# A two-layer recurrent and attention backbone: separate banks for the last gates, and output projections that open with the rounded parts of two row tiles

## The reference, cut to what matters

```python
# layer 0
z = h @ w_in                                   # (T, 1024) @ (1024, 2048)
g_ = gelu(z[..., :D]);  xc = conv4(z[..., D:])
for d in (0, 1):                               # forward, backward
    g = einsum('btnk,gnkj->gbtnj', xc_blocks, gate_w[d]) + gate_b[d]
    r, ig = sigmoid(g[0]), sigmoid(g[1])
    log_a = -8 * r * softplus(-lam[d])
    h_t = exp(log_a) * h_t-1 + sqrt(-expm1(2 * log_a)) * (ig * xc)
o = (sum_over_d(h) * g_) @ w_out
# layer 1
o = attention_heads(512 x 1024) @ w_o
# both
x = x + gate1 * o
hn = modulate(rmsnorm(x), shift, scale)
aff = softmax(hn @ router);  gate, idx = top_k(aff.T, cap)     # per expert
x = x + gate2 * scatter(gate * swiglu(hn[idx], w_up[e], w_down[e]))
```

## Time and profile before

| | before |
|---|---|
| median of 3 runs | 1846.26 us (1844.49 to 1847.72) |
| the profiled execution | 1847.21 us |
| its span in the profile | 1845.5 us |
| mean granted TensorE clock | 0.972 of 2.4 GHz |
| TensorE matmul busy | 1687.3 us (91%) |
| VectorE busy | 710.8 us (39%) |
| ScalarE busy | 528.3 us (29%) |
| loads and stores | 520.56 MB, mean 282 GB/s |
| last recurrent unit, first projection and choice of rows | 239 to 383 us of the span |
| experts of layer 0 | from 383 us |
| last attention values, second projection and choice | 1282 to 1377 us |
| experts of layer 1 | from 1377 us |

### The profile page before, as it was taken

One profiled execution on the slowest core, in us unless ns is written; L12 is line 12 of the kernel. 1 busy time (PEld: TensorE's weight loads), 2 busy tenths in 40 slices (PEclk: granted clock), 3 DMA queues, 4 the chain that ended last, 5 costly groups with the idle time before them and its releaser, 6 DMA issues. The chain is left out here.

```text
span 1845.5 us, 23947 instructions
## 1 busy us (share of the span) xinstructions
PE 1687.3 (91%) x9811; PEld 882.4 (48%) x9811; DVE 710.8 (39%) x1431; ACT 528.3 (29%) x885; POOL 181.1 (10%) x198
## 2 busy tenths in 40 slices
PE   4999989879999999999988999999959998888887
PEld 2667768533333333333358778777833332222222
DVE  4667765611221221221145655665451221122123
ACT  4677783300110110110144445446210000000002
POOL 1000010100001000010011225324000000000001
PEclk8999999979999999999999999999979999999999
DMA  9554351699999999999881000000579999999996
GB/s 360 190 206 163 140 220 64 263 386 407 397 404 391 399 403 385 403 404 385 342 300 50 22 1 0 0 0 34 210 308 421 421 420 422 421 421 421 421 422 258
DMA packets 89577, 520.56 MB, mean 282 GB/s; under 512 B 11347, under 2 KB 19648, under 8 KB 33936
## 3 DMA queue, kind: packets, MB, share of 16 engines
q1 hardware_dynamic: 80128, 487.74, 65.6%
q0 software_dynamic: 9360, 31.54, 5.5%
HBM read 502.37 MB, written 16.88 MB: 281 GB/s over the span
## 5 line engine op out<-in xcount | busy, mean ns | idle before, releaser
L847 PE MATMUL wide<-sb_ring_x,sb_xT 128*64 128x512 f32 x1160 | 266.6, 601 | 19.8 <-DMA sb_ring_x<-moe_w_up 18.7
L847 PE MATMUL wide<-sb_ring,sb_xT 128*64 128x512 f32 x888 | 204.5, 603 | 14.4 <-DMA sb_ring<-moe_w_up 12.2
L847 PEld LDWEIGHTS wide<-sb_ring_x,sb_xT 128*64 128x64 f32 x1160 | 78.0, 137 | 190.1 <-issue 136.9
L847 PEld LDWEIGHTS wide<-sb_ring,sb_xT 128*64 128x64 f32 x888 | 60.9, 138 | 146.3 <-issue 108.8
L902 PE MATMUL duo<-sb_ring_x,sb_hidT 128*64 128x512 f32 x536 | 124.3, 599 | 4.4 <-DMA sb_ring_x<-moe_w_down 4.4
L1832 DVE TENSOR_TENSOR sb_hid<-wide,sb_sg 128x512 f32<-128x512 f32 x16 | 11.1, 692 | 304.3 <-ACT sb_sg_c L1365 304.3
L2281 POOL TENSOR_TENSOR sb_prob<-sb_prob,sb_asum 128x768 f32<-128x768 f32 x64 | 93.9, 1468 | 186.4 <-DVE sb_asum L2105 186.4
L902 PE MATMUL duo<-sb_ring,sb_hidT 128*64 128x512 f32 x424 | 99.9, 601 | 7.2 <-DMA sb_ring<-moe_w_down 7.1
L1363 ACT ACTIVATE sb_sg<-wide 128x512 f32<-128x512 f32 x16 | 9.6, 597 | 335.7 <-PE wide L858 335.7
L1832 DVE TENSOR_TENSOR sb_hid<-wide,sb_hid 128x512 f32<-128x512 f32 x16 | 11.1, 691 | 227.1 <-ACT sb_hid L1363 227.1
L1363 ACT ACTIVATE sb_hid<-wide 128x512 f32<-128x512 f32 x16 | 9.6, 598 | 278.5 <-PE wide L847 278.5
(11 more groups left out here) (389 smaller groups left out, 2866.4 us busy)
## 6 DMA issues: line engine op xcount, KB each, us to landing
sb_ring_x<-moe_w_up SPq DMA_DIRECT2D x145, 1024.0 KB, 25.0
sb_ring<-moe_w_up SPq DMA_DIRECT2D x111, 1024.0 KB, 24.4
sb_ring_x<-moe_w_down SPq DMA_DIRECT2D x69, 1024.0 KB, 23.0
sb_ring<-moe_w_down SPq DMA_DIRECT2D x59, 1024.0 KB, 23.9
sb_ring<-ada_w SPq DMA_DIRECT2D x40, 1024.0 KB, 7.0
sb_ring<-lru_w_in SPq DMA_DIRECT2D x8, 1024.0 KB, 8.2
sb_ring_x<-ada_w SPq DMA_DIRECT2D x8, 1024.0 KB, 7.5
sb_ring<-lru_w_out SPq DMA_DIRECT2D x4, 1024.0 KB, 4.9
```

Source lines behind the costliest of these rows:

```text
L847: ins = mm(wide[n * CAPL:(n + 1) * CAPL, s, :], mine[:, k, :], w[:, at:at + BANK], start=k == 0, stop=k == KD - 1)
```

## The change

The last block's plan puts both gates ahead of its ada chunks. Unit 15's gates go to `wide` banks 2, 3 and 0, without waiting for unit 14's sigmoids (the last product waits for gelu 6, which reads bank 0), and the last input projection goes to the two banks of `turned`, after unit 14's sigmoids. The warming products are 20, not 46.

Both output projections begin with `first_two`: rounded by rounded products of tiles 0 and 1, block by block as rounded weights come; then the products of the row tiles' rests, tile 0 and tile 1; then those of the weights' rests, tile 0 and tile 1. The last block (two blocks in layer 1) of the rounded tiles is made apart, so that the others need not wait for the last Y (or heads). Product 2 is now cut in two, with tile 0's turning between; from product 3 on the order is as it was. The slots of the up projections are given back by turnings into `turned`, without the wait for the heads.

```diff
@@ plan @@
-        plan += [("gate", n, 0)] + beside[0:3] + [("gate", n, 1)] + beside[3:]
+        if n < KD - 1:
+            plan += [("gate", n, 0)] + beside[0:3] + [("gate", n, 1)] + beside[3:]
+        else:
+            plan += [("gate", n, 0), ("gate", n, 1)] + beside
@@
+        EARLY_K = [KD - 1, KD - 2]
+        def in_banks(p):
+            if p == 2 * KD - 1:
+                return turned[:, 0, :], turned[:, 1, 0:TC]
+            return wide[:, 2 * (p % 2), :], wide[:, 2 * (p % 2) + 1, 0:TC]
+
+        def gate_banks(u):
+            if u == 2 * KD - 1:
+                return wide[:, 2, :], wide[:, 3, :], wide[:, 0, :]
+            return turned[:, 0, :], turned[:, 1, :], duo[:, 0, :]
@@ in_project @@
-                if p >= 2:
+                if p == 2 * KD - 1:
+                    pe.wait_ge(s_sig, p)
+                elif p >= 2:
@@ gates @@
-                if u >= 1:
+                if 1 <= u < 2 * KD - 1:
                     pe.wait_ge(s_sig, u)
...
+                if u == 2 * KD - 1:
+                    pe.wait_ge(s_gelu, KD - 1)
+                mm(i_lat, w[:, KD + n, :], seg(xc, 0), start=True, stop=True).then_inc(s_gmm, 1)
@@ out_project @@
+                def first_two():
+                    lhs, w = [out_lhs(lay, t) for t in range(2)], [out_w(lay, k) for k in range(KD)]
+                    for k in range(KD):
+                        pe.wait_ge(s_whi, W0[lay] + k + 1)
+                        if k == EARLY_K[lay]:
+                            pe.wait_ge(s_hhi, L0[lay] + 2)
+                        for t in range(2):
+                            for n in range(2):
+                                mm(wide[:, 2 * t + n, :], lhs[t][1][:, k, :], w[k][1][:, n * BANK:(n + 1) * BANK], start=k == 0, stop=False)
+                    for t in range(2):
+                        pe.wait_ge(s_hlo, L0[lay] + t + 1)
+                        for k in range(KD):
+                            for n in range(2):
+                                mm(wide[:, 2 * t + n, :], lhs[t][2][:, k, :], w[k][1][:, n * BANK:(n + 1) * BANK], start=False, stop=False)
+                    for t in range(2):
+                        for k in range(KD):
+                            if t == 0:
+                                pe.wait_ge(s_wlo, W0[lay] + k + 1)
+                            for n in range(2):
+                                ins = mm(wide[:, 2 * t + n, :], lhs[t][1][:, k, :], w[k][2][:, n * BANK:(n + 1) * BANK],
+                                         start=False, stop=k == KD - 1)
+                        ins.then_inc(s_o[lay], 1)
...
+                first_two()
+                product(2, 0, 4)
+                turn_tile(s, 0)
+                product(2, 4, KD)
+                turn_tile(s, 1)
...
+                logit_products(0)
+                product(3, 0, KD)
+                turn_tile(s, 2)
+                logit_products(1)
+                turn_logits(0)
@@ after the plan @@
-            idle_products(duo[:, 0, :], 46)
+            idle_products(duo[:, 0, :], 20)
@@ after the attention loop @@
-            pe.wait_ge(s_OT, 2 * NG + 2)
...
-                turn(duo[0:32, 1, 32 * n:32 * n + 32], ident[0:32, 0:32]).then_inc(used[place[name][0]], 1)
+                turn(turned[0:32, 0, 32 * n:32 * n + 32], ident[0:32, 0:32]).then_inc(used[place[name][0]], 1)
@@ norm_and_logits, ScalarE @@
-                out_weights_hi(lay, 0, 1)
-                if lay == 0:
-                    act.wait_ge(s_yg, KD)
-                else:
-                    act.wait_ge(s_OT, 2 * NG + 2)
-                out_lhs_hi(lay, 0)
-                out_weights_hi(lay, *range(2, KD))
-                out_lhs_hi(lay, 1)
+                ready, last, early_w = ((s_yg, KD - 1), (s_yg, KD), 5) if lay == 0 else ((s_OT, 2 * NG), (s_OT, 2 * NG + 2), 3)
+                act.wait_ge(*ready)
+                for t in range(2):
+                    x_, hi, _ = out_lhs(lay, t)
+                    fn(hi[:, 0:EARLY_K[lay], :], x_[:, 0:EARLY_K[lay], :], ACT.Copy)
+                out_weights_hi(lay, *range(early_w))
+                act.wait_ge(*last)
+                for t in range(2):
+                    x_, hi, _ = out_lhs(lay, t)
+                    fn(hi[:, EARLY_K[lay]:KD, :], x_[:, EARLY_K[lay]:KD, :], ACT.Copy).then_inc(s_hhi, 1)
+                out_weights_hi(lay, *range(early_w, KD))
@@ residual_norm, VectorE @@
-                out_weights_lo(lay, 0)
+                out_weights_lo(lay, 0, 1)
                 out_lhs_lo(lay, 0)
-                out_weights_lo(lay, *range(1, KD))
                 out_lhs_lo(lay, 1)
+                out_weights_lo(lay, *range(2, KD))
```

More of the change, by code:

```diff
@@ L571, in idle_products, with ada_chunk @@
                     mm(bank[:, 0:P], ident[:], ident[:], start=True, stop=True)
-            def ada_chunk(i, k, owed=None):
+            def ada_chunk(i, k, *owed):
+                owed = [d for d in owed if d is not None]
                 if i >= 1 and k == 0:
@@ L583, in ada_chunk @@
                              start=k == 0, stop=k == KD - 1)
-                    if owed and n == 0:
-                        ins.then_inc(owed, 1)
+                    if n < len(owed):
+                        ins.then_inc(owed[n], 1)
                 ins.then_inc(used[place[("ada", i, k)][0]], 1)
@@ L638, in in_project @@
                 pe.wait_ge(s_wlo, p + 1)
-                b = 2 * (p % 2)
+                banks = in_banks(p)
                 for k in range(KD):
@@ L644, in in_project @@
                         for i in range(2):
-                            ins = mm(wide[:, b, :] if i == 0 else wide[:, b + 1, 0:TC], w[:, p % 2, k, :], seg(h[:, k, :], i),
+                            ins = mm(banks[i], w[:, p % 2, k, :], seg(h[:, k, :], i),
                                      start=k == 0 and n == 0, stop=k == KD - 1 and n == 2)
@@ L672, in _ @@
                 if what == "in":
-                    in_project(*at, last, owed)
-                    owed = None
+                    in_project(*at, last, *owed)
+                    owed = []
                 elif what == "gate":
                     gates(*at)
-                    owed = last
+                    if last is not None:
+                        owed.append(last)
                 elif what == "ada":
-                    ada_chunk(*at, owed)
-                    owed = None
+                    ada_chunk(*at, *owed)
+                    owed = []
                 else:
@@ L732, in turn_logits @@
                     turn(duo[:, 1, 0:P], logit_parts[:]).then_inc(s_logt, 1)
-                if lay == 0:
-                    for t in range(4):
-                        product(t, 0, KD)
-                        if t >= 1:
-                            turn_tile(s, t - 1)
-                        if t == 2:
-                            pe.wait_ge(s_modcol, 4)
-                        if t >= 2:
-                            logit_products(t - 2)
-                        if t == 3:
-                            turn_logits(0)
+                first_two()
[3 more added lines that the diff above has]
+                turn_tile(s, 1)
+                if lay == 0:
+                    pe.wait_ge(s_modcol, 4)
+                else:
+                    pe.wait_ge(s_OT, 2 * NG + 2)
+                logit_products(0)
[3 more added lines that the diff above has]
+                turn_logits(0)
+                if lay == 0:
                     product(4, 0, 4)
@@ L777, in out_project @@
                     return
-                for step in range(n_t + 3):
-                    if step < n_t:
-                        product(step, 0, KD)
-                    if 1 <= step <= n_t:
-                        turn_tile(s, step - 1, *(() if step < n_t else [used[place[names[3]][0]]] + [used[j] for j in WO_SLOTS]))
-                    if 2 <= step <= n_t + 1:
-                        logit_products(step - 2)
-                    if step >= 3:
-                        turn_logits(step - 3)
+                turn_tile(s, 3, *([used[place[names[3]][0]]] + [used[j] for j in WO_SLOTS]))
+                logit_products(2)
+                turn_logits(1)
+                logit_products(3)
+                turn_logits(2)
+                turn_logits(3)
             def turn_choice(lay):
@@ L1249, in _ @@
                         act.wait_ge(s_yg, (u - 3) // 2 + 1)
-                    for g, lat, dst in ((1, duo[:, 0, :], IT), (0, turned[:, 0, :], RT)):
+                    r_lat, ctx_, i_lat = gate_banks(u)
+                    for g, lat, dst in ((1, i_lat, IT), (0, r_lat, RT)):
                         bias = pB[:, B_GB + (2 * d + g) * KD + n:B_GB + (2 * d + g) * KD + n + 1]
                         fn(seg(dst[:, u % 3, :], 0), lat, ACT.Sigmoid, bias=bias)
-                        ins = fn(seg(dst[:, u % 3, :], 1), turned[:, 1, g * TC:(g + 1) * TC], ACT.Sigmoid, bias=bias)
+                        ins = fn(seg(dst[:, u % 3, :], 1), ctx_[:, g * TC:(g + 1) * TC], ACT.Sigmoid, bias=bias)
```

(6 more changed lines are left out.)

15 lines of the change are left out of this document (6 added, 9 removed).

## The result

The changed kernel takes **1834.91 us** (median of 4 runs, 1834.40 to 1835.16), beside it the kernel before took 1846.87 us; the ratio is 0.9937, interval 0.992 to 0.9954. Forecast were 1836.1 us and a range of 1833.5 to 1840.0. The profiled execution took 1835.05 us for a span of 1833.3.

The account below looks back on a forecast made before the run. No one engine bounds the kernel; expert stages start when the projections before them end, where engines wait in turn. 6.7 us (first layer) plus 3.5 (second) gives 10.2, so 1846.26 - 10.2 = 1836.1 us; range 1833.5 to 1840.0.

Parts of the forecast that it names:

- The bound: Both expert stages: neither is shortened, but each starts as much earlier as the output projection and choice of rows end.
- Nothing passes: Rival, both layers: the choices of rows wait for something other than the projection; time stays at 1846; chance 0.05.
- the second start being worth nothing: Rival, second layer's projection: none of its 3.5 us passes, gain 6.7 us, time 1839.6; chance 0.12.
- The last unit: Last recurrent unit: unit 15's sigmoids, waiting for Y of block 6, start at 249.87 not 252.59; 2.7 us, not 4.7.
- The first projection, its start: First layer's output projection: TensorE begins at 266.15, after the first rounded weight at 266.1, and follows ScalarE's pace.
- The wait before product 2: First layer's output projection: product 2 waits 0.2 us for tile 0's residual and tile 2's rest.
- The first projection, its clock: First projection: cutting warming products from 46 to 20 leaves a 2.6 us gap; clock loss taken as 0.
- the rival: Clock falls at the first projection, costing 1.1 us: gain 9.1 us, time 1837.2; chance 0.18.
- The second projection: Second layer's output projection: starts at 1285.6 not 1288.57, tile 1 turned 3.5 us earlier, 1.5 of it from the clock.
- The load of weight 6: Second projection: load of weights 6 and 7, issued 0.9 earlier and asked for at 1290.8, may cost some tenths.
- Slower: Rival, first projection: first pair runs at 1.2 GHz throughout, 12 us slower, 1858; chance 0.02.

Follow-up runs that it names:

- second projection alone: Kernel before with the new order only in the second layer's output projection, its five dummy turnings placed earlier, 46 warming products kept: 1841.64 us, ratio 0.9978.
- the gates alone: Kernel before with only the last unit's gate banks and order new, old projections and 46 warming products: 1841.51 us, ratio 0.9982.
- early sigmoids: Changed kernel, unit 15's sigmoids waiting for block 6's scan, not its Y; 20 warming products: 1831.05 us, ratio 0.9924; once more 1834.04 us, 0.993.
- the changed kernel's third: Changed kernel measured a third time, no edit: 1834.90 us, ratio 0.9942 to the kernel before.
- early sigmoids with 26: Changed kernel, unit 15's sigmoids waiting for block 6's scan instead of its Y, 26 warming products in place of 20: 1831.35 us, ratio 0.991.

## Why the prediction was right, and where not

**The bound.** Right: the gain passes through both expert stages. From the first up product of layer two to the end it is 468.1 before and 467.8 changed, 467.6 to 468.0 in all but two of the other profiles (469.3 and 469.4 in those). In the first layer the first up product came at 376.22 for 383.35, 7.1 earlier, of which 2.46 are the start. "Nothing passes" falls, and so does the second start being worth nothing, with 3.4 to 3.6 in it in each of the nine profiles of the new order without a late load.

**The last unit.** Right to some hundredths: 2.70 for 2.72 forecast, the sigmoids behind Y of block 6, and not the 4.7 that the gates alone would give. The run without this wait shows the other 2.1. The slow gate products that the prediction read in the earlier trace rows come with a fall of the clock: in all three profiles with the old gates it fell during TensorE's wait of 4.3 us there or just after it; with the new gates, whose last product waits 0.88 to 1.04, in none of ten.

**The first projection, its start.** Forecast were 16.28 us from the sigmoids to the first product, measured 16.33. The wait before product 2: 0.2 forecast, 0.18 measured. Without a fall of the clock the pair and product 2 take 34.95 (32 warming products) where 35.25 were forecast.

**The first projection, its clock.** This step failed, inside a forecast that came out right. I took 0 for the cut of the warming products, with the argument that the gap is a single one behind dense products, as that of 1.8 us is. The clock fell in all four profiles with a gap of 2.70 or 2.71, and the gap of 1.8 was no safe model either: with the second projection alone it fell behind that one too. It cost 1.1 us against 32 products, the number kept as the price of the rival (1.1). That rival had a chance of 0.18 and is what happened; its loss was made up by terms set a little too low (0.3 in the products, 0.1 in the second layer) and by scatter. The local parts alone would have given 1846.26 - 9.6 = 1836.7; that the median came out 1.2 below the forecast, and not 0.6 above it, is luck. The local parts give 9.6, the rival said 9.1, the forecast 10.2; the three measurements of the changed kernel gave 12.0, 9.1 and 10.9.
Counted over all profiles at this place, the clock was low at the first products once in one behind a gap of 7.17, four times in four behind 2.70, once in two behind 2.52 and 2.53, once in three behind 1.80, and never in three behind 1.19 or without a gap. So a longer gap makes the fall likelier; where between 1.19 and 2.70 it becomes safe, so few profiles can't say.
The Trainium skill, TensorE: Matmul & The Clock Gate, asks in the table of its section "Why this matters for your kernels" that no idle gap exceed about 3 us. The runs don't bear it out as a safe bound, since most of the falls counted here came behind shorter gaps. The measurements decide.

**The second projection.** Right: 3.63 for 3.5. First product 0.20 after the values for 0.35 forecast, product 2 after 23.15 for 23.1, its turning after 12.0 for 12.0. Of the 3.63, 3.12 come from the earlier start and 0.51 from what follows it; how much of it the clock gives, put at 1.5, no run isolates. The clock stayed at 1.00 here in all eleven profiles with the new order, and fell in both with the old. The load of weight 6, named as the one place that might cost some tenths, landed before it was asked for in the changed kernel (three profiles), and cost 1.26 and 0.69 with 32 warming products. Before, and with the gates alone, it cost 0.31 and 0.52, so the old order has such waits as well.

**Slower.** The pair did not stay at 1.2 GHz: it was low for some 3.4 us of its 24, and even with no warming products for 5.4. The price of a whole pair at half clock never came near.

## What to carry to other kernels

When a chain of waits loses one, look for the wait that is next on the same engine before counting the gain: here the sigmoids waited for Y, though a scan had freed what they overwrite 5 us before Y was done, and setting it right was worth 2.1 us (from there on the sigmoids of unit 14, on the same engine, are what they follow), nearly as much as the new banks. When work that only keeps the clock up is cut, let it end where the next real product can start; 26 products in place of 20 cost nothing, and in their one profile the clock held, which is worth the 1.1 us that the cut had given away. For gains below 0.5%, measure the length between two events around the change in several profiles: it repeated to 0.1 us as long as the clock did the same (58.01, 58.11, 58.13) and moved by 1.1 when it didn't (54.90, 55.98), where medians of five runs of one kernel moved by 3 (1831.05, 1834.04, on two chips).

## What the runs showed of the hardware that was not expected

**The clock's fall is partly chance, and goes with the largest part of the scatter between profiles.** The stretch from the first up product of layer one to the end of the values of layer two is the same program in all kernels here. It took 901.9 us before, 901.1 changed, but 897.6, 897.0 and 897.5 in three of the thirteen profiles (second projection alone, early sigmoids, the changed kernel's third). Lining up the instructions with those of the kernel before puts 3.6 to 4.0 of the 4.3 to 4.9 us at 940 to 1020 us, in attention. Busy tables, first of the kernel before, then of early sigmoids:
```profile
940.00:980.00 40.00, 35.44 (x256) 33.04 (x245) 21.13 (x45) 22.64 (x49) 6.05 (x11) 0.91 0.60 216
980.00:1020.00 40.00, 33.31 (x187) 30.28 (x186) 22.39 (x78) 15.36 (x40) 4.61 (x18) 0.83 0.22 80
```
```profile
940.00:980.00 40.00, 36.62 (x257) 36.02 (x257) 22.68 (x57) 25.35 (x62) 6.61 (x20) 1.00 0.46 179
980.00:1020.00 40.00, 32.73 (x166) 25.55 (x165) 23.42 (x85) 11.32 (x26) 1.16 (x6) 0.87 0.22 79
```
Time at full clock lost in these 80 us: (1 - 0.91) x 40 + (1 - 0.83) x 40 = 10.4 us before, 5.2 in the other; the stretch from up product to values is 4.9 shorter, 4.0 of it here. Over all thirteen, 5.2 lost goes with 897.0 to 897.6, 7.0 to 8.6 with 899.1 to 899.9 (not in strict order: 7.0 goes with 899.9), and 10.2 to 10.4 with 901.1 to 901.9. No edit here touches that place, so a single profile can be 5 us off for this alone, half of what the change is worth. Whole runs show the same: among the six of early sigmoids with 26, two with a mean granted clock of 0.981 took 1824.88 and 1825.66, the other four, at 0.973 to 0.976, took 1830.98 to 1833.26. That the clock causes the difference is not shown by an edit; they go together. And not all scatter goes with it: from the turning of tile 1 to the first up product of layer one the thirteen profiles take 74.9 to 78.0, the old orders as much as the new, and the clock lost there doesn't follow these lengths.

**One load, two landing times.** The load of weights 6 and 7 of the second output projection leaves right after the values in all kernels with the new order, ahead of the experts' loads, and ScalarE asks for it some 5.2 us later. It was there in time in nine of eleven profiles, and 1.26 and 0.69 late in the two with 32 warming products. In both, the next four loads took longer to issue as well, 2.69 and 3.06 against 1.88 to 2.08 in the nine. Whether the 32 products have a part in it or two of eleven is chance stays open; no run held the load apart from those that follow it.
